# Two norms of a transformer kernel worked by halves of the tokens, with the output tile in front and the first weight slots behind

## What is computed

```python
def rms_norm(x, w):
    y = xf * lax.rsqrt(jnp.mean(xf * xf, axis=-1, keepdims=True) + EPS)
    return y * w

def modulate(x, w, shift, scale):
    return rms_norm(x, w) * (1 + scale) + shift

h = modulate(x, norm_w[0], ...);  x = x + 0.5 * gate0 * swiglu(h, ffn_w13[0], ffn_w2[0])
h = modulate(x, norm_w[1], ...);  x = x + gate1 * hybrid_mixer(h, ...)
h = modulate(x, norm_w[2], ...);  x = x + 0.5 * gate2 * swiglu(h, ffn_w13[1], ffn_w2[1])
```

## Time and profile before

| | us |
|---|---|
| device time, median of 3 runs | 2285.34 (2284.29 to 2286.47) |
| device time of the profiled execution | 2284.05 |
| its span, first to last instruction | 2282.0 |
| PE busy | 2243.5 (98%) |
| DVE busy | 1455.3 (64%) |
| ACT busy | 929.6 (41%) |
| POOL busy | 415.1 (18%) |
| mean granted TensorE clock | 0.998 |

### The profile page before, as it was taken

The page is one execution under the profiler, slowest core; times in us unless marked ns, Lnnn a source line. Parts: engine busy times, 40 slices in busy tenths (PEclk is TensorE's granted clock), DMA queues, the critical chain, the costliest instruction groups (busy, mean ns, idle before and its releaser), DMA issues. The chain is left out here.

```text
span 2282.0 us, 38417 instructions
## 1 busy us (share of the span) xinstructions
PE 2243.5 (98%) x14842; PEld 1848.0 (81%) x14842; DVE 1455.3 (64%) x1953; ACT 929.6 (41%) x1523; POOL 415.1 (18%) x516
## 2 busy tenths in 40 slices
PE   7999999999999999999999999999999999899998
PEld 5888888677787788888888888888888887788887
DVE  5766544766444766644557677666677678757767
ACT  4332322644433422233434554444444554552234
POOL 0111000000000111100033344333333334101102
PEclk9999999999999999999999999999999999999999
DMA  8776643221232667633221112112112112222222
GB/s 307 248 233 219 195 145 106 74 83 57 70 100 94 222 217 229 218 115 107 94 66 57 56 48 67 64 57 66 57 57 65 57 57 65 61 84 97 87 92 74
DMA packets 70338, 255.05 MB, mean 112 GB/s; under 512 B 7600, under 2 KB 7856, under 8 KB 70192
## 3 DMA queue, kind: packets, MB, share of 16 engines
q1 hardware_dynamic: 52048, 186.87, 25.6%
q0 software_dynamic: 18144, 66.08, 8.7%
HBM read 250.83 MB, written 2.10 MB: 111 GB/s over the span
## 5 line engine op out<-in xcount | busy, mean ns | idle before, releaser
L317 DVE TENSOR_TENSOR wl<-raw,wh 128x1024 fp32r<-128x1024 f32 x331 | 418.4, 1265 | 407.4 <-ACT wh L312 404.2
L321 PE MATMUL ps<-hH,wh 128*128 128x512 f32 x1640 | 655.6, 400 | 4.0 <-issue 2.3
L323 PE MATMUL ps<-hH,wl 128*128 128x512 f32 x1640 | 639.7, 390 | 0.0
L322 PE MATMUL ps<-hL,wh 128*128 128x512 f32 x1640 | 638.7, 389 | 0.0
L312 ACT ACTIVATE wh<-raw 128x1024 fp32r<-128x1024 f32 x331 | 348.2, 1053 | 228.9 <-PE ps L323 224.0
L321 PEld LDWEIGHTS ps<-hH,wh 128*128 128x128 f32 x1640 | 308.0, 188 | 72.4 <-issue 9.7
L323 PEld LDWEIGHTS ps<-hH,wl 128*128 128x128 f32 x1640 | 307.8, 188 | 65.8
L322 PEld LDWEIGHTS ps<-hL,wh 128*128 128x128 f32 x1640 | 308.3, 188 | 63.5 <-issue 3.4
L2060 POOL TENSOR_TENSOR XR<-XR,fp 128x512 f32<-128x512 f32 x112 | 147.6, 1318 | 525.4 <-ACT KQ L1740 468.0
L731 POOL DMA_DIRECT2D araw<-in_ada x120 | 63.9, 533 | 822.3 <-DVE aacc L745 385.5
L745 DVE SCALAR_TENSOR_TENSOR aacc<-araw,cols,aacc 128x1024 f32<-128x1024 f32 x115 | 147.5, 1283 | 9.2 <-DVE aacc L745 1.2
(11 more groups left out here) (402 smaller groups left out, 3607.2 us busy)
## 6 DMA issues: line engine op xcount, KB each, us to landing
raw<-in_ws SPq DMA_DIRECT2D x331, 512.0 KB, 3.5
araw<-in_ada POOLq DMA_DIRECT2D x120, 512.0 KB, 4.8
praw<-in_ada SPq DMA_DIRECT2D x8, 1024.0 KB, 16.4
xin<-in_x SPq DMA_DIRECT2D x2, 1024.0 KB, 7.3
out_x<-xout SPq DMA_DIRECT2D x3, 512.0 KB, 2.6
cin<-in_ctx POOLq DMA_DIRECT2D x1, 1024.0 KB, 5.3
mask<-in_mask POOLq DMA_DIRECT2D x1, 512.0 KB, 3.6
traw<-in_dfts POOLq DMA_DIRECT2D x1, 512.0 KB, 3.7
```

The lines of the kernel that those rows point to most:

```text
L317: dve.tensor_tensor(wl[:, j, :], raw[:, j, :], wh[:, j, :].bitcast(F32), ALU.subtract).then_inc(lo_ready, 1)
L321: pe.matmul(o, a_hi, b_hi, start=start, stop=False, **kw)
L322: pe.matmul(o, a_hi, b_lo, start=False, stop=False, **kw)
L323: return pe.matmul(o, a_lo, b_hi, start=False, stop=stop, **kw)
```

## The change

Both norms are done for tokens 0 to 255 (FRONT) and then for tokens 256 to 511 (BACK).

- The last output tile is made twice with 256 columns, first the front half over all its slots, then the back half; the slots are released in the second pass only. DVE adds each half to `xT`, ACT squares each half.
- The ones matmuls of the front half stand inside the back half of that tile (`front_mean_pe`), those of the back half inside the front half of the pair (`back_mean_pe`). `spin_pe` is gone.
- The pair of slots is worked twice with 256 columns (`pair_columns_pe`). In seam 2 the third slot too (`single_columns_pe`): pair front, single front, pair back, single back.
- The scaled tile of the front half is made by other engines: ACT copies x * gain into a scratch (`gained_act`, 8 copies of 256 columns: in `araw` at seam 1, in `m1` at seam 2), and POOL multiplies the copy with `rs` (`front_scaled_pool`). DVE keeps the low parts. The back half is made as before by DVE and ACT, with 256 columns.
- ACT and DVE orders are written anew, among them the splits of `B0` and `B0 + 1`, which stand between the front tiles now.
- POOL's DMA for the positions and the loads of the second feed-forward stand behind its 8 multiplications and wait for the back half's `rs`.

The diff, cut to its core:

```diff
-        def spin_pe(pe, bank, s, n=12):
...
+        def pair_columns_pe(pe, banks, s, m, half, between=None):
+            cols, first = (FRONT, BACK)[half], TILES_AT[m] + 8 * half
+            slot_ready(pe, s)
+            slot_ready(pe, s + 1)
+            for k in range(KD):
+                if between is not None and k == 2:
+                    between(pe)
+                w = slice(k * P, (k + 1) * P)
+                pe.wait_ge(nh_done, first + k + 1)
+                for u in range(2):
+                    j, o = (s + u) % RING, ps[:, banks[u], cols]
+                    pe.matmul(o, wh[:, j, w], hH[:, k, cols], ...)
+                    pe.matmul(o, wl[:, j, w], hH[:, k, cols], ...)
+                pe.wait_ge(nl_done, first + k + 1)
...
+        def gained_act(act, m, gained, ks):
+            for k in ks:
+                act.activation(gained(k), xT[:, k, FRONT], ACT.Copy, scale=gain[:, k:k + 1])
+        def front_scaled_pool(pool, m, gained):
+            first = TILES_AT[m]
+            pool.wait_ge(rs_step, ROOTS_AT[m] + 2)
+            for k in range(KD):
+                if k >= 2:
+                    pool.wait_ge(nl_done, first + k - 1)
+                pool.tensor_tensor(nt[:, k % 2, FRONT], gained(k), rs[:, FRONT], ALU.mult).then_inc(nt_done, 1)
...
+        def back_norm_dve(dve, m, shift):
+            dve.wait_ge(rs_step, ROOTS_AT[m] + 4)
+            dve.wait_ge(nt_done, TILES_AT[m] + 8)
+            back_scaled_dve(dve, m, 0)
+            for k in range(KD):
+                if k + 1 < KD:
+                    back_scaled_dve(dve, m, k + 1)
+                half_low_dve(dve, m, shift, 1, (k,))
...
+        def ffn_last_tile_pe(pe, s, banks):
+            for half, cols in enumerate((FRONT, BACK)):
+                for w in range(W2S):
...
+                        if half and k == 4:
+                            front_mean_pe(pe, 1, 4)
+                    if half:
+                        last.then_inc(slot_done, 1)
+                if half == 0:
+                    last.then_inc(front_out, 1)
...
+        def mix_norm_act(act):
+            act.wait_ge(gain_done, 2)
+            act.wait_ge(ada_step, 8 * KD + ADA_RING)
+            gained_act(act, 1, gained_mix, range(KD - 1))
+            half_square_act(act, 1, KD + 2, FRONT)
+            gained_act(act, 1, gained_mix, (KD - 1,))
+            half_rms_act(act, 1, 4, 0)
+            half_high_act(act, 1, shift, 0, (0, 1))
+            split_hi(act, B0)
+            half_high_act(act, 1, shift, 0, (2, 3))
+            split_hi(act, B0 + 1)
+            half_high_act(act, 1, shift, 0, (4,))
+            half_square_act(act, 1, KD + 3, BACK)
+            half_high_act(act, 1, shift, 0, (5, 6, 7))
+            half_rms_act(act, 1, 7, 1)
+            split_hi(act, B0 + 2)
+            half_high_act(act, 1, shift, 1, range(KD))
...
+        def ffn2_norm_act(act):
+            act.wait_ge(gain_done, 3)
+            act.wait_ge(gb_l, KD)
+            gained_act(act, 2, gained_ffn2, range(KD - 1))
+            half_square_act(act, 2, 2 * KD + 3, FRONT)
+            gained_act(act, 2, gained_ffn2, (KD - 1,))
...
         def mix_pe(pe):
-            norm_pe(pe, 1, 4)
-            spin_pe(pe, 0, B0)
-            gemm_pair(pe, (0, 1), B0, 8).then_inc(slot_done, 2)
+            pair_columns_pe(pe, (0, 1), B0, 1, 0, lambda e: back_mean_pe(e, 1, 7))
+            pair_columns_pe(pe, (0, 1), B0, 1, 1).then_inc(slot_done, 2)
...
-                gemm_pair(pe, (0, 1), s0, 8 * m).then_inc(slot_done, 2)
-                for p in range(1, 3):
-                    ffn_pair_pe(pe, i, s0, p, 0)
+                pair_columns_pe(pe, (0, 1), s0, m, 0, lambda e: back_mean_pe(e, m, 4))
+                single_columns_pe(pe, 2, s0 + 2, FRONT)
+                pair_columns_pe(pe, (0, 1), s0, m, 1).then_inc(slot_done, 2)
+                single_columns_pe(pe, 2, s0 + 2, BACK).then_inc(slot_done, 1)
+                gemm(pe, ps[:, 3, :], s0 + 3, 0, 6, hH, hL).then_inc(slot_done, 1)
+                ffn_pair_pe(pe, i, s0, 2, 0)
```

More of the change, by code:

```diff
@@ L17 @@
 T, TC = 512, 256
+TH = T // 2
 D = 1024
@@ L358, in gemm_pair @@
             return last
-        def spin_pe(pe, bank, s, n=12):
-            slot_ready(pe, s)
-            for _ in range(n):
-                pe.matmul(ps[:, bank, :], wh[:, s % RING, 0:P], wh[:, s % RING, 0:T], start=True, stop=True)
         def norm_pe(pe, m, bank, n=T):
@@ new lines, in back_mean_pe, with half_square_act @@
+        def back_mean_pe(pe, m, bank):
+            pe.matmul(ps[:, bank, BACK], const("ones"), acc[:, BACK], start=True, stop=False, skip_group_check=True)
+            pe.wait_ge(sq_done, SQUARES_AT[m] + 9)
+            pe.matmul(ps[:, bank, BACK], const("ones"), sq[:, BACK], start=False, stop=True,
+                      skip_group_check=True).then_inc(ms_done, 1)
+        def half_square_act(act, m, r, cols):
+            act.wait_ge(acc_step, 8 * m + 8)
+            act.wait_ge(resid, r)
+            act.activation(sq[:, cols], xT[:, KD - 1, cols], ACT.Square).then_inc(sq_done, 1)
@@ L992, in mix_pe @@
                     pe.wait_ge(gb_m, KD)
+                if o == KD - 1:
+                    for half, cols in enumerate((FRONT, BACK)):
+                        if half:
+                            pe.wait_ge(resid, 2 * KD)
+                        for k in range(KD):
+                            c = slice(k * P, (k + 1) * P)
+                            last = products(pe, ps[:, (6, 7)[half], cols], wh[:, s % RING, c], wl[:, s % RING, c], mH[:, k, cols],
+                                            mL[:, k, cols], k == 0, k == KD - 1, skip_group_check=True)
+                            if half and k == 4:
+                                front_mean_pe(pe, 2, 3)
+                        last.then_inc((front_out, slot_done)[half], 1)
+                    break
                 for k in range(KD):
```

172 lines of the change are left out of this document (136 added, 36 removed).

## The result

The changed kernel takes **2293.99 us**, the median of 7 runs (2292.81 to 2295.35), beside 2285.91 (7 runs, 2284.29 to 2287.78) for the kernel before. The ratio is 1.0036, with a 95% interval from 1.0027 to 1.0046: slower by 0.36%, some 8 us. The forecast was 2289.0 and its range ended at 2292.5.

What follows compares the result with a forecast made beforehand. PE, busy 98% at full clock, was taken to bound the kernel. Seam 1's +0.9 and seam 2's +2.8 made +3.7 us on 2284.05, so 2287.8; with the median 1.3 above, 2289.0, range 2284.8 to 2292.5.

Steps and rivals of the forecast that it cites:

- The bound: Whole kernel: PE is busy 98% of the span at full clock; 5.87 us pass without a product at each seam.
- the chain: At each seam, before the first product: tile 7, addition, square, mean, Ln, Exp, scaled tile, high part.
- the line between 0.40 and 1.05: Both front halves: POOL's 256-column multiplication priced at 0.62 us, between least times at 128 and 512 columns.
- no exclusion: Front halves: low parts and POOL's tiles overlap, 0.9 us a tile, -0.7 and +1.5 at the seams, 2286.1; chance 0.17.
- +2.8 forecast: Seam 2: the fourth slot starts at about 766.25 instead of 763.42, 2.8 us later.
- +0.9 forecast: Seam 1: the pair's last two products end at 416.95, against the single slot's start at 416.01 before, 0.9 us later.
- Eight tiles by 1.13 are 9.0: Seam 1 front half: eight tiles of POOL's multiplication and DVE's low part in turn, 1.13 us each, take 9.0.
- 2 x 1.14: Seam 1 front half: DVE's splits of `B0` and `B0 + 1` lie between the front tiles, 1.14 us each.
- The clock, the slower side: Both seams: PE idleness brings 3 us at half clock, costing 1.5 us at seam 2, 2290.5; chance 0.15.
- At seam 1 the back half is DVE's pace, 0.2 slack a tile, and hides it: Seam 1 back half: DVE's tile pace hides the 1.5 us of PE's work lost to half clock.
- PE runs almost without idleness behind both seams, so nothing absorbs it: Behind both seams: the summed delay of +3.7 us passes into the kernel's time in full.
- a slow POOL: Front halves: POOL's tile takes 1.05, the cycle is 0.43 longer, 3.4 us at each seam, 2296; chance 0.10.

## Why the prediction was wrong

**What held.** The bound, the chain and most prices. Front tiles of both seams are 1.08 to 1.10 us apart (POOL starts at 401.14 and 402.22, at 754.77 and 755.87), 1.13 forecast. That term was right in part by luck: POOL's tile takes 0.74 and not the 0.62 of the line between 0.40 and 1.05, but the low part ends 0.28 behind it and not 0.48. POOL and DVE exclude each other, which was the choice against *no exclusion*. Seven copies take 2.90 us, 0.40 apart (0.37 taken), and PE waits 2.01 (2.0 forecast) and 1.40 (1.4) at seam 2. The fourth slot is 2.84 later, +2.8 forecast. Back tiles at seam 1 follow every 0.92.

**Seam 1, +0.9 forecast, +1.6 at full clock.** The step that failed is a term of the sum, "Eight tiles by 1.13 are 9.0" with "2 x 1.14" for DVE's splits of `B0` and `B0 + 1`. The exclusion was charged to the low parts and not to the splits, and it works both ways. Behind the split of `B0` POOL's fourth tile took 1.80, so ACT's fourth high part and its split of `B0 + 1` came late:

```profile
400.81 0.51 ACT L477 ACTIVATE hH<-nt,cols 128x256 fp32r<-128x256 f32 x1 [1.49 <-POOL nt L490]
401.23 1.04 ACT L314 ACTIVATE wh<-raw 128x1024 fp32r<-128x1024 f32 x1
```

That is 17.10 behind tile 7 in place of 16.7, and it puts DVE's split of `B0 + 1` 0.35 late. This split then took 1.73 in place of 1.23, since a POOL tile started 0.08 before it (402.22 and 402.30). So PE starts 20.16 behind tile 7 in place of 19.19 and stands 3.23 in place of 2.4. Behind the split DVE makes the addition of the back half, which holds it for 0.40 (403.95 to the next low part at 404.35) and stood in the sum at nothing. The last front low part ends 23.65 behind tile 7 (22.9 forecast). The end of the seam follows by the same 0.7.

**The clock.** *The clock, the slower side* was a rival at 0.15, priced at 1.5 us at seam 2, with "At seam 1 the back half is DVE's pace, 0.2 slack a tile, and hides it". That sentence failed, and so did the term that it put at nothing. The pace of the back tiles hides what slows them; it can't hide what delays their start, and the mean of the back half stands on PE inside the stretch that runs slow. It cost 1.25 at seam 1 in the first profile, behind an idle spell of 3.23 (2.29 in the earlier trace rows), and 0.5 at seam 2 in the one profile where it fell there.

**Seam 2 ends later than I looked.** This is the largest step that failed, 1.55 us. The forecast took the fourth slot as the end of the seam and said that "PE runs almost without idleness behind both seams, so nothing absorbs it". Nothing absorbs it, but something adds to it: the fifth slot is late by 4.39 where the fourth is by 2.84. I had costed the pair's late release only through the fourth slot's split. The sums and the product stood in no row that I had read, as they were off the path before; they had 10.69 - 8.6 = 2.1 us less notice now. Moving the sums brought 1.43 back.

**The sum.** 1.6 + 4.4 = 6.0 at full clock, where 3.7 were forecast. The two medians of the changed kernel lie 8.1 and 7.9 over those of before beside them, so some 2 us remain. The clock's 1.25 in some executions and the 0.6 to 1.3 of the Fourier mixer are of that size; how they share it isn't shown. The rival *a slow POOL* (2296) was nearer in number but not in mechanism: POOL's tile alone takes 0.72, not 1.05.

## What to carry to other kernels

When work is released later but all else stays, look one and two uses further than the first: what was queued behind a long wait before, at no cost, is now on the path, and moving it behind the next producer alone only moves the wait to another queue. Splitting elementwise work over DVE and POOL bought nothing here, where both read two SBUF operands; the version on one engine was 6 us faster, two of them by the copies that went with it and perhaps one by the clock. The same exclusion can show up far from the change, wherever the two engines' instructions shift against each other. Spins in front of a waiting matmul engine are not idle decoration: in the kernel before they were worth 3 to 4 us.

## What the runs showed of the hardware

A half clock behind an idle spell of 3.2 us came in three of six profiled executions, once in the two of the same program, so one profile neither convicts nor clears it. With the exclusion, DVE's `scalar_tensor_tensor` of 256 columns stretched from 0.48 to 0.96, its split from 1.23 to 1.73, and POOL's tile from 0.72 to 1.80: by 0.48, 0.50 and 1.08, where the other's instruction had 0.68, 0.64 and 1.20 left. A split beside a POOL multiplication of 1024 columns (2.40) took 1.96 when it started 1.56 behind it and 3.29 when it started 0.20 behind it. POOL's multiplication of 256 columns takes 0.72 to 0.75 by itself, above the 0.62 of the line between its least times at 128 and 512 columns.
